# Router logits taken before the norm is applied, five more early places for expert weights, and a pair's way down moved behind the next pair's way up

## The reference, cut to what matters

```python
x = x + mix
x = x + hier_moe(rms_norm(x, norm_ffn_g[l]), ...)
return rms_norm(x, norm_final_g)

def hier_moe(h, ...):
    g_logits = hf @ w_group + b_group            # 4 groups
    grp = argmax(g_logits); p_grp = softmax(g_logits)[grp]
    e_logits = (hf @ w_expert + b_expert)        # 32 experts, those of the group count
    top_v, top_i = lax.top_k(e_in, 2)
    weight = p_grp * softmax(top_v)
    # every token goes through its 2 experts:
    # (silu(x @ w_gate_e) * (x @ w_up_e)) @ w_down_e, 1024 -> 256 -> 1024
```

## Time and profile before

| | us |
|---|---|
| median of 3 runs | 3193.94 (3193.71 to 3194.86) |
| the profiled execution, whole | 3193.26 |
| its span in the trace | 3191.1 |
| mixer's last residual chunk ready | 2879.9 |
| first product of pair 0 starts, ends | 2925.3, 2934.2 |
| last product of pair 15 ends | 3160.6 |

### The profile page before, as it was taken

How to read it: one execution, slowest core, us unless ns; L and a number is a source line. 1 busy time by engine, 2 the same in 40 slices (tenths; PEclk the granted TensorE clock), 3 DMA queues, 4 the chain that set the end, 5 groups by cost and what they waited for, 6 DMA issues and landing times.

```text
span 3191.1 us, 32848 instructions
## 1 busy us (share of the span) xinstructions
PE 3020.4 (95%) x13352; PEld 2200.5 (69%) x13352; DVE 1420.8 (45%) x3127; ACT 472.8 (15%) x1040; POOL 314.8 (10%) x303
## 2 busy tenths in 40 slices
PE   9999999979999999999999799999999988997985
PEld 7886444946888866888864448888855566885321
DVE  7563311434555334554346826554333056663113
ACT  1101010001001021001022221001021075012101
POOL 0000100111000100000111230000100084001110
PEclk9999999689999999999999899999999999998998
DMA  5222222102222212222212012222212300227996
GB/s 206 80 82 84 86 79 81 39 27 73 93 93 80 94 65 106 93 79 93 93 54 79 30 40 99 79 93 93 93 66 106 119 28 22 85 93 298 425 425 282
DMA packets 54348, 345.46 MB, mean 108 GB/s; under 512 B 7984, under 2 KB 8112, under 8 KB 15536
## 3 DMA queue, kind: packets, MB, share of 16 engines
q1 hardware_dynamic: 44496, 319.84, 26.5%
q10 hardware_dynamic: 5088, 15.06, 1.2%
q0 software_dynamic: 4608, 8.40, 0.7%
HBM read 336.97 MB, written 14.68 MB: 110 GB/s over the span
## 4 chain that ended last, share of the span: by engine, by line
PE 87%; DVE 5%; DMA 4%; ACT 1%; issue 1%; SPq 1%; POOL 0%; ACTq 0%; DVEq 0%; POOLq 0%
PE bank L832 52%; PE bank L483 18%; PE bank L492 4%; PE bank L1466 2%; PE bank L2668 2%; DMA ring<-in_weights 2%; PE bank L519 1%; PE bank L513 1%; PE bank L1718 1%; PE bank L1702 1%; PE bank L1493 1%; DVE area L1763 1%; DMA buf_b<-in_weights 1%; PE bank L2685 1%; DMA norm<-in_weights 1%
## 5 line engine op out<-in xcount | busy, mean ns | idle before, releaser
L483 PE MATMUL bank<-area,ring 128*128 128x512 f32 (+1 forms) x964 | 335.1, 509 | 19.6 <-DVE area L1596 15.6
L832 PE MATMUL bank<-buf_b,mixed 128*128 128x256 f32 x1472 | 334.3, 379 | 0.0
L832 PE MATMUL bank<-area,mixed 128*128 128x256 f32 x1504 | 333.7, 379 | 0.0
L854 DVE TENSOR_TENSOR mixed<-ring 128x512 f32<-128x512 f32 (+2 forms) x144 | 96.0, 666 | 506.8 <-PE bank L832 500.1
L832 PE MATMUL bank<-buf_a,mixed 128*128 128x256 f32 x1408 | 319.8, 379 | 0.0
L832 PEld LDWEIGHTS bank<-area,mixed 128*128 128x128 f32 x1504 | 285.8, 190 | 38.9
L832 PEld LDWEIGHTS bank<-buf_b,mixed 128*128 128x128 f32 x1472 | 279.7, 190 | 38.0
L483 PEld LDWEIGHTS bank<-area,ring 128*128 128x128 f32 x964 | 163.4, 191 | 188.3 <-issue 169.3
L832 PEld LDWEIGHTS bank<-buf_a,mixed 128*128 128x128 f32 x1408 | 267.6, 190 | 36.8 <-DVE mixed L862 0.4
L832 PE MATMUL bank<-buf_b,ring 128*128 128x256 f32 x1184 | 271.5, 379 | 0.4 <-ACT buf_b L712 0.4
L832 PE MATMUL bank<-buf_a,ring 128*128 128x256 f32 x1056 | 244.1, 380 | 7.9 <-DMA buf_a<-in_x 7.5
(11 more groups left out here) (392 smaller groups left out, 3289.9 us busy)
## 6 DMA issues: line engine op xcount, KB each, us to landing
ring<-in_weights SPq DMA_DIRECT2D x241, 1024.0 KB, 4.8
area<-in_weights SPq DMA_DIRECT2D x27, 1024.0 KB, 29.1
buf_a<-in_weights SPq DMA_DIRECT2D x11, 1024.0 KB, 28.0
buf_b<-in_weights SPq DMA_DIRECT2D x10, 1024.0 KB, 28.5
mixed<-in_weights SPq DMA_DIRECT2D x6, 1024.0 KB, 28.2
norm<-in_weights SPq DMA_DIRECT2D x6, 1024.0 KB, 28.0
area<-chosen SPq DMA_DIRECT2D x8, 512.0 KB, 7.4
buf_a<-in_x ACTq DMA_DIRECT2D x4, 512.0 KB, 7.4
```

The lines of the kernel that those rows point to most:

```text
L483: mm = pe.e.matmul(bank[0:w.shape[1], 0:n], w, x[k], start=k == 0, stop=k == len(pieces) - 1)
L832: mm = pe.e.matmul(b, w[:, k * P:(k + 1) * P], x(INPUT_OF[p], unit.lo + k), start=(unit.key, BANK_OF[p]) not in begun, stop=unit.last and ...
L854: made = tt(unit.mix("S1"), unit.quarter("A21"), unit.quarter("A22"), ALU.add)
```

## The change

Five edits. (1) The router's weights are multiplied by the gain once, on DVE, ahead of the mixer's output products (`vector_router_weights`), into a tile `router_w` with 64 columns a chunk. Logits are then products of the plain residual with `router_w` standing, each chunk as soon as `nsa_out` allows, between the folds of the squares; they come out as 64 x 256 twice, are copied, turned, and on DVE scaled by the token's number and given the bias in one instruction a block of tokens. (2) The normalised tokens in `buf_b`, their spreading and their turning to rows go. The turned residual is kept for the sum and, scaled by token on ACT, is what the table in memory holds; the gain is multiplied in when gathered rows are turned, now on DVE. (3) `rank` takes 8 products instead of 14, and the weights of the experts (`r_comb`) are worked out behind `slotted`. (4) With `buf_b` and parts of `area` and `const` free, `COMMON` has 13 homes: five of them (`EARLY`) are filled behind the mixer's last merge product, and `HOMES` has 18. (5) A pair's way down stands behind the next pair's way up and its turn; blocks are packed in that order, and three gathers are issued ahead instead of two.

```diff
                                for name in ("w_gate_e_2", "w_up_e_2")] for half in range(2) for e in (2 * p, 2 * p + 1)]
-        plan[f"moe{p}_down"] = [[("w_down_e_2", (0, e), ((k * P, P),), ((n * T, T),))
-                                 for k in range(EFF // P) for n in range(D // T)] for e in (2 * p, 2 * p + 1)]
+        if p:
+            plan[f"moe{p - 1}_down"] = expert_down_pieces(p - 1)
+    plan[f"moe{NEXP // 2 - 1}_down"] = expert_down_pieces(NEXP // 2 - 1)
     return plan
...
+    def tensor_route(pe, stream, r):
+        st = "nsa"
+        square, raw = opened(pe, g, ("squares", st)), opened(pe, g, ("raw",))
...
+        def logits(k):
+            pe.wait_ge(nsa_out, k + 1)
+            for half in range(2):
+                mm = pe.e.matmul(raw[64 * half:64 * (half + 1), 0:T // 2], router_w[:, k, :], r[:, k, half * (T // 2):(half + 1) * (T // 2)],
+                                 start=k == 0, stop=k == KD - 1)
+            return mm
+        pe.wait_ge(squares_summed, SUMMED[st] + KD - 1 - LATE[st])
+        fold(pe, square, square_sums, start=True)
+        pe.wait_ge(router_scaled, 2)
+        for k in range(2):
+            logits(k)
+        squares_late(pe, st, square, KD - 2)
+        for k in range(2, 4):
+            logits(k)
+        end(g, squares_late(pe, st, square, KD - 1), ("squares", st))
+        for k in range(4, KD):
+            mm = logits(k)
+        end(g, mm, ("raw",))
+        out = opened(pe, g, ("inverse",))
+        pe.wait_ge(inverted, STATS[st] + 1)
+        end(g, transpose(pe, out[:, 0:P], scale_c), ("inverse",))
+        out = opened(pe, g, ("logits",))
+        pe.wait_ge(raw_copied, 1)
+        for c in range(2):
+            mm = transpose(pe, out[:, c * P:(c + 1) * P], raw_logits[:, c * P:(c + 1) * P])
+        end(g, mm, ("logits",))
+        for b in range(TB):
...
-        x = cols(h)
-        tensor_turn_residual(pe, r, XT_SCALE)
-        tokens_product(pe, stream, g, [("router", b) for b in range(TB)], plan["router"][0], x, NGRP + NEXP, ready)
-        for b in range(TB):
-            tensor_turn_tokens(pe, g, "xr", h, b)
...
-        for b in range(TB):
-            for c in range(b + 1):
-                pe.e.matmul(out[:, b * NEXP:(b + 1) * NEXP], C("before") if c == b else C("ones"), r_both[:, c, :],
-                            start=c == 0, stop=c == b)
+        every = r_both.rearrange("p b e -> p (b e)")
+        pe.e.matmul(out[:, 0:TB * NEXP], C("before"), every, start=True, stop=False)
+        for c in range(1, TB):
+            pe.e.matmul(out[:, c * NEXP:TB * NEXP], C("ones"), every[:, 0:(TB - c) * NEXP], start=False, stop=c == TB - 1)
...
+    def scalar_route(ac):
+        scalar_rms_sqrt(ac, "nsa")
+        ac.e.dma_start(gain, io["gain"]).then_inc(gain_loaded, 16)
+        ac.wait_ge(*g.done(("raw",)))
+        ac.e.activation(raw_logits, bank(("raw",))[:, 0:T // 2], ACT.Copy).then_inc(raw_copied, 1)
+        for b in range(TB):
             for half in range(2):
...
-        def rows(b):
-            scalar_turn_tokens(ac, "xr", xrows, xrows_done, (b,))
-            ac.wait_ge(xrows_done, 2 * b + 2)
...
+            ac.wait_ge(inverse_read, 1)
+            ac.e.activation(xrows[b], xt[b], ACT.Copy, scale=inverse[:, b:b + 1]).then_inc(xrows_done, 1)
+            ac.wait_ge(xrows_done, b + 1)
             ac.e.dma_start(tokens_dram[b * P:(b + 1) * P, :], xrows[b]).then_inc(tokens_stored, 16)
...
+    def vector_router_weights(ve):
...
+        w = ring[:, at:at + KD * (NGRP + NEXP)].rearrange("p (k n) -> p k n", k=KD)
+        for lo, hi, to in ((0, NGRP, 0), (NGRP, NGRP + NEXP, 8)):
+            ve.e.tensor_tensor(router_w[:, :, to:to + hi - lo], w[:, :, lo:hi],
+                               S("ffn_g").unsqueeze(2).to_broadcast([P, KD, hi - lo]), ALU.mult).then_inc(router_scaled, 1)
...
+        vector_inverse(ve, "nsa")
...
+        cp(inverse, bank(("inverse",))[:, 0:P:32]).then_inc(inverse_read, 1)
...
+            stt(r_logit[:, b, :], bank(("logits",))[:, at:at + ROUTED], inverse[:, b:b + 1], router_bias, ALU.mult,
+                ALU.add).then_inc(logit_read, 1)
+        ve.wait_ge(logit_read, TB)
...
-    COMMON = IN_RING[:-1] + [(flat_mixed, x_loaded[0], 1), (region(6144, BLOCK), x_loaded[1], 1), (region(21504, BLOCK), x_loaded[2], 1),
-                             (norm[:, :], x_loaded[3], 1)] + IN_RING[-1:]
-    HOMES = COMMON + [(flat_a[:, 0:BLOCK], const_loaded, 1), (flat_a[:, BLOCK:2 * BLOCK], small_loaded, 1),
-                      (flat_b[:, 0:BLOCK], pos_loaded, 1), (flat_b[:, BLOCK:2 * BLOCK], p_loaded, 2),
-                      (region(2048, BLOCK), half_loaded[0], 0), (region(4096, BLOCK), half_loaded[1], 0), (region(0, BLOCK), half_loaded[2], 0)]
+    spare = const_at["steps"][0] + SLOTS
+    EARLY = [(region(0, BLOCK), x_loaded[0], 1), (region(BLOCK, BLOCK), x_loaded[1], 1), (flat_b[:, 0:BLOCK], x_loaded[2], 1),
+             (flat_b[:, BLOCK:2 * BLOCK], x_loaded[3], 1), (const[:, spare:spare + BLOCK], const_loaded, 1)]
+    COMMON = IN_RING[:1] + EARLY + IN_RING[RING - 1:] + IN_RING[1:RING - 1] + [(flat_mixed, small_loaded, 1), (norm[:, :], pos_loaded, 1)]
+    HOMES = COMMON + [(flat_a[:, 0:BLOCK], p_loaded, 2), (flat_a[:, BLOCK:2 * BLOCK], turn_loaded[0], PPC // 2),
+                      (region(6144, BLOCK), turn_loaded[1], PPC // 2), (region(8192, BLOCK), table_stored, PPC), (region(TABLES, BLOCK), s5_loaded, 4)]
     def home(block, homes):
...
+            if k == 0:
+                sy.wait_ge(tensor_groups, g.reader[FIRST - RING])
+            elif k == 1:
+                for way in ("ga", "gb", "pa", "pb"):
+                    sy.wait_ge(*g.done((("square", "b", way, KD // 2 - 1), 0, PARTS[-1])))
+            elif k == 1 + len(EARLY):
+                sy.wait_ge(router_scaled, 2)
+            elif k < len(COMMON) - 2 and k > 1 + len(EARLY):
+                sy.wait_ge(tensor_groups, g.reader[FIRST + k - 1 - len(EARLY) - RING])
+            elif k == len(COMMON) - 2:
                 sy.wait_ge(nsa_out, KD)
-            elif k == len(COMMON) - 2:
+            elif k == len(COMMON) - 1:
                 sy.wait_ge(*g.done(("squares", "nsa")))
-            elif k == len(COMMON) - 1:
-                sy.wait_ge(tensor_groups, g.reader[FIRST - 1])
-            load_home(sy, block, COMMON)
+            load_home(sy, FIRST + k, COMMON)
...
+        turn(0)
+        for p in range(EP):
+            up(p)
+            if p + 1 < EP:
+                turn(p + 1)
+            if p:
+                down(p - 1)
+            hidden_turn(p)
+        down(EP - 1)
...
             if k == len(COMMON) + 2:
-                sy.wait_ge(xrows_done, 2 * TB)
+                sy.wait_ge(tokens_stored, 16 * TB)
+                sy.wait_ge(rows_in_loaded[0], 16)
             elif k == len(COMMON) + 4:
-                sy.wait_ge(tokens_stored, 16 * TB)
-            elif k == len(COMMON) + 6:
-                sy.wait_ge(slotted, 1)
+                sy.wait_ge(comb_ready, 1)
             elif k >= len(HOMES):
                 sy.wait_ge(tensor_groups, gs.reader[block - len(HOMES)])
             load_home(sy, block, HOMES)
@@ -2705,21 +2775,11 @@
                 sy.e.dma_start(ys[2 * b + i], chosen_dram[at:at + P, :]).then_inc(landed[2 * b + i], 16)
     def scalar_slots(ac, gs):
-        def turned(p):
-            for half in range(2):
-                ac.wait_ge(*gs.done(("xturn", p, half)))
-                if p > 1:
-                    ac.wait_ge(*gs.done(("up", p - 2)))
-                ac.e.activation(xs_turned[p % 2][:, half * T:(half + 1) * T], bank(("xturn", p, half), gs), ACT.Copy).then_inc(xs_done, 1)
-        turned(0)
         for p in range(EP):
...
+                ve.e.tensor_tensor(chunks(xs_turned[p % 2][:, half * T:(half + 1) * T], 4), chunks(bank(("xturn", p, half), gs), 4),
+                                   S("ffn_g", 4 * half, 4 * half + 4).unsqueeze(2).to_broadcast([P, 4, P]), ALU.mult).then_inc(xs_done, 1)
...
+        turned(0)
+        for p in range(EP):
+            ve.wait_ge(e_silu, p + 1)
+            ve.e.tensor_tensor(e_hidden[p % 2], e_hidden[p % 2], bank(("up", p), gs)[:, EFF:2 * EFF], ALU.mult).then_inc(e_mul, 1)
+            if p + 1 < EP:
+                turned(p + 1)
+            if p:
+                rows(p - 1)
+            ve.wait_ge(*gs.done(("hturn", p)))
+            if p > 1:
+                ve.wait_ge(*gs.done(("ed", p - 2, 1)))
+            ve.e.tensor_copy(e_turned[p % 2], bank(("hturn", p), gs)[:, 0:2 * P]).then_inc(turned_back, 1)
+        rows(EP - 1)
...
-        for p in range(2):
+        for p in range(3):
             bring(p)
         for p in range(EP):
-            if p + 2 < EP:
-                bring(p + 2)
+            if p + 3 < EP:
+                bring(p + 3)
```

(16 more changed lines are left out.)

203 lines of the change are left out of this document (98 added, 105 removed).

## The result

The changed kernel takes 3172.5 us (median of four runs, 3171.1 to 3173.7) against 3193.8 beside it; the ratio is 0.9935, with a 95% interval from 0.9922 to 0.9947. In two later comparisons it had 0.9932 (0.9918 to 0.9945) and 0.9937 (0.9924 to 0.9951). 3170 was forecast, in a range of 3163 to 3180. The span of the profiled execution falls from 3191.1 to 3169.3 us, by 21.8; 23.6 were reckoned.

The account below looks back on a forecast made before the run. DMA bytes were taken to set the end once pair 0's way up ends. Gains of 20.0 us up to there, 3.1 for bytes and 0.5 at the end, 23.6 from 3193.26, gave 3169.7, stated as 3170; range 3163 to 3180.

Parts of the forecast that it names:

- X: End of pair 0's way up, 2934.2 before the change; forecast at 2914.2, 20.0 us earlier.
- What bounds the kernel: Pair loop: DMA bytes set its end at 422 GB/s, TensorE hides behind them; levers are X and bytes left then.
- Part 1: Residual to logits: logits between the folds, spreading and normalising gone; picking starts at 2885.1, gain 12.2 us.
- Part 2: Picking to table: `rank` starts behind picking and takes 1.2 us; gain 3.2 us, `slotted` at 2896.5.
- Part 3: Token rows: ACT takes 2.6 us a block, last store lands 2897.6, 1.1 us behind `slotted`; gather starts 2898.8.
- Part 4: First gather: lands in 4.5 us instead of 9.98, gain 5.5; turn and way up of pair 0 take 10.8.
- rival A: First gather: its 10 us are its own, so X is 5.5 us later, 3175.3 us; chance 0.17.
- Part 5: After X: one block and one scatter less save 3.1 us; the loop's new order saves 0.5 at the end.
- B: Token rows later: ACT 3.3 us a block, last store 5 us; 5.2 us later, 3175 us; chance 0.12.
- C: Early blocks held up until 2881, gather behind them, X about 2924: 3179 us; chance 0.05.
- D: Pair loop: TensorE's clock stays at its lower level; ten such pairs give 3262 us; chance 0.02.

Follow-up runs that it names:

- e3: Changed kernel with the loop's old order, a pair's way down right behind its own hidden turn: 3173.77 us, ratio 0.9937.
- e1: Changed kernel without SP's wait that holds the last three homes' blocks until the first gather has landed: 3176.21 us, ratio 0.9948.
- e10: Changed kernel with SP holding all five homes' blocks, `buf_a`'s two included, until the first gather has landed: 3174.32 us, ratio 0.9943.
- e4: Kernel before the change, with SP holding the last five of seven homes' blocks until the first gather has landed: 3191.24 us, ratio 0.9993.
- e5: Changed kernel with idle products (11, 7 and 22) in three gaps of TensorE, ahead of `rank`, table and first turn: 3174.84 us, ratio 0.9946.
- e6: Changed kernel with POOL's clearing after picking, and VectorE copying the last pair's hidden turn ahead of the previous pair's rows: 3172.25 us, ratio 0.9938.
- e8: Changed kernel with the edits of e5 and e6 together: 3172.83 us, ratio 0.9936.
- e9: As e8 on the changed kernel, but with 10 idle products ahead of the first turn of gathered rows instead of 22: 3170.84 us, ratio 0.9930.
- e12: Changed kernel again without edits, timed beside e9, e10 and e11: 3172.08 us, ratio 0.9937.
- e11: Changed kernel with the five early blocks held until the residual is ready and placed behind the ring's blocks: 3180.59 us, ratio 0.9960.
- e2: Changed kernel with the five early blocks held until the residual's end, four ring blocks held behind them: 3186.01 us, ratio 0.9977.
- e0: Changed kernel again without edits, timed beside e1, e2 and e3: 3171.36 us, ratio 0.9932.

## Why the prediction was right

The mechanism was right: the end is set by bytes behind X, and X by one chain. The closeness of the sum (21.8 measured, 23.6 reckoned) is in part luck: X is 3.3 us later than forecast, 1.1 us more than forecast was gained behind it, and the gather's time was hit with a wrong make-up. By its own steps, counted in the profile after:

- **What bounds the kernel** held: full transfers from X on, and X set by one chain. e3 shows no gain of the loop's order beyond the end; e1 moves X by 3.7 to 5.1 us and the time by 4.9. e10 and e4, where blocks are on their way at X, show that the bytes left count as much as X.
- **Part 1**, picking at 2885.1: 2886.12. The logits of a chunk took 0.48 us, the table load lay beside the folds as forecast. 11.2 us gained for 12.2; 0.4 of the difference is the residual itself, ready at 2880.3 in this execution for 2879.9.
- **Part 2** was the mis-sized term. Picking took 5.7 for 5.0 (the cast beside POOL's memset). `rank` took 3.6 for 1.2: 2.0 is its time at full clock (e5), so 0.8 of the miss was its size; the rest is the lower level, which the prediction had weighed for the turns of tokens but not for `rank`, 3.3 us of idle TensorE behind them. The turns themselves ended at 2888.7, for 2888.3. So `slotted` was at 2900.76 for 2896.5.
- **Part 3**: 2.67 us a block for 2.6. The last store was issued at 2896.0 for 2895.0 and took 2.9 us, or 3.7 where `buf_a` went out with it, for 2.6. (The 5.0 us are the first store's, issued at 2888 beside the last of the 13 blocks; it has landed long before the last one.) So the stores let the gather go at 2900.9 where the placing was ready (e1, e5, e6, e8, e9, e12). In the profile after the placing was 1 us later still, and the gather was released by it and not, as forecast, by a store. Forecast 2898.8, measured 2901.94.
- **Part 4**: 4.55 for 4.5, rival A (10) false by e1 and e10. Turn and way up took 10.9 for 10.8. X is 3.3 us late, 3.1 of it from the gather's issue.
- **Part 5**: from X to the last transfer some 217 us, as said. X to the last product shrank by 4.7 us (226.4 to 221.7) for 3.6, what follows it by 0.4. The sum closes: 16.7 + 4.7 + 0.4 = 21.8, for 20.0 + 3.1 + 0.5. Of the 1.1 us more up to the last product, the prediction overlooked 0.6: with three gathers issued ahead of the loop a fourth goes out ahead of X (2909.27), so 12 fall behind X and not 13, 0.26 MB less. The rest wasn't traced.
- Of the rivals, B (token rows later, X some 5 us late) was wrong by its own terms: ACT takes 2.67 us a block, not 3.3, and the last store 2.9 to 3.7 us, not 5. The delay that is here came from picking and `rank`. C's price was put at 9 us for early blocks that are not early; e11 measured 8.5. D is out: the clock stands at 1.00 through the loop.
- Not shown by a run of its own: the router's part (edits 1 to 3), the largest term of the sum. It is read from the two chains of waits; no run had the old router beside the new homes.

## What to carry to other kernels

Where bytes set the end, reckon with the DMA engines' idle time ahead of the full stretch and with the bytes left at its start, not with the chain alone: e4 had X 5.9 us earlier and ended 2.6 to 3.8 us earlier. A small transfer on which everything waits, a gather or the stores ahead of it, should find the other queues empty; three large blocks in them doubled the gather's time. Moving a wait on the queue that issues in order moves all that stands behind it.

## What the runs showed of the hardware

- A gather of 0.26 MB took 4.6 us alone (e10), 4.6 to 5.7 with the tail of two blocks beside it, 8.4 to 10.0 beside a full queue (e2, e1, before); token stores of 0.5 MB took 2.6 to 5.0 us, and 8.5 to 12.3 beside a full queue (e2, e11).
- The landing of the gather, counted from picking, fell between 2906.27 and 2906.53 in nine executions, whether it was issued at 2900.9 or 2901.9 and whether `buf_a` was beside it. No run settles why these give one time.
- TensorE needs 6.1 to 6.8 us from the table's last product to the first one behind the branch (e5, e8, e9). In the profile after it is 6.9, so an earlier landing alone would have gained 0.1 to 0.8 us.
- The clock's fall is not at a fixed place: `rank` behind 3.3 us of idle TensorE took 3.6 us in the profile after and 2.9 in e0, with its first four products (eight passes) still at full clock.
